# Dense attention with its softmax pairs joined one step earlier, squares taken tile by tile, and an output projection that opens two columns at once

## The reference

```
s = einsum(q, k) * d ** -0.5 ; causal                 # dense: 4 heads, each a pair of maps
p = softmax(s)
a = p[:, :, 0] - lam * p[:, :, 1]                      # the pair is joined
o = einsum(a, v)
y_c = rms(o, d_out_g) * (1 - lam_init)
merged = g0 * (y_a @ w0) + g1 * (y_b @ w1) + g2 * (y_c @ w2)
x = x + merged @ w_out
```

## Time and profile before

| | |
|---|---|
| median of three runs | 3001.89 us (3000.51 to 3002.13) |
| the profiled execution | 2999.98 us, its span 2998.2 us |
| granted TensorE clock | 0.998 of full speed |
| PE busy | 2944.5 us, 98% of the span |
| DVE, ACT, POOL busy | 1494.7, 674.4, 2001.7 us |
| PE in the chain that ended last | 91% |
| dense loop, layer 0 | about 276 to 382 us from the start, layer 1 about 1208 to 1313 |
| opening of the output projection | from 540.0 us, and from 1471.5 us |

### The profile page before, as it was taken

The page is one execution under the profiler, slowest core; times in us unless marked ns, Lnnn a source line. Parts: engine busy times, 40 slices in busy tenths (PEclk is TensorE's granted clock), DMA queues, the critical chain, the costliest instruction groups (busy, mean ns, idle before and its releaser), DMA issues.

```text
span 2998.2 us, 37823 instructions
## 1 busy us (share of the span) xinstructions
PE 2944.5 (98%) x13886; PEld 2402.7 (80%) x13886; DVE 1494.7 (50%) x2573; ACT 674.4 (22%) x1490; POOL 2001.7 (67%) x2041
## 2 busy tenths in 40 slices
PE   8999999999999999999999999999999999999998
PEld 6887777888888887777888888878888888888886
DVE  7778884533324788775543322566321231424543
ACT  3265354200001345345110000100111121211000
POOL 6775545777777767454777777887776556565775
PEclk9999999999999999999999999999999999999999
DMA  4321222333233322211433333233333223222332
GB/s 146 99 91 58 71 67 67 127 99 97 94 96 126 101 85 85 64 64 60 130 94 95 98 95 103 91 99 95 97 93 106 78 85 99 78 85 78 98 98 71
DMA packets 86922, 274.37 MB, mean 92 GB/s; under 512 B 10368, under 2 KB 11008, under 8 KB 86784
## 3 DMA queue, kind: packets, MB, share of 16 engines
q1 hardware_dynamic: 85248, 270.44, 29.1%
q10 hardware_dynamic: 1536, 2.10, 0.3%
HBM read 266.21 MB, written 4.19 MB: 90 GB/s over the span
## 4 chain that ended last, share of the span: by engine, by line
PE 91%; DVE 7%; ACT 1%; issue 1%; POOL 0%; DMA 0%; DVEq 0%; SPq 0%; ACTq 0%; POOLq 0%
PE PS L501 59%; PE PS L539 14%; PE PS L810 5%; PE PS L818 3%; PE PS L576 1%; PE PS L856 1%; PE PS L868 1%; PE PS L1107 1%; PE PS L897 1%; DVE SQ L1779 1%; PE PS L590 1%; PE PS L880 1%; DVE SMALLS L1744 0%; PE PS L1082 0%; PE PS L1094 0%
## 5 line engine op out<-in xcount | busy, mean ns | idle before, releaser
L471 POOL TENSOR_TENSOR WL<-RAW,WH 128x512 fp32r<-128x512 f32 (+2 forms) x538 | 803.4, 1493 | 9.8
L463 POOL TENSOR_TENSOR POOL_C<-POOL_C 128x1 f32<-128x1 f32 x538 | 127.1, 236 | 928.0 <-PE PS L501 517.7
L501 PE MATMUL PS<-XNH,WH 128*128 128x512 f32 (+1 forms) x1712 | 674.2, 394 | 1.5 <-DVE TMP L2342 1.2
L501 PE MATMUL PS<-XNL,WH 128*128 128x512 f32 (+1 forms) x1712 | 666.9, 390 | 0.0
L468 POOL TENSOR_TENSOR WL<-RAW,WH 128x512 fp32r<-128x512 f32 x420 | 578.1, 1377 | 35.0
L464 POOL TENSOR_SCALAR WH<-RAW 128x1024 fp32r<-128x1024 f32 (+3 forms) x538 | 533.4, 991 | 0.5 <-issue 0.3
L501 PE MATMUL PS<-XNH,WL 128*128 128x512 f32 (+1 forms) x1712 | 423.3, 389 | 0.1
L501 PEld LDWEIGHTS PS<-XNH,WH 128*128 128x128 f32 (+1 forms) x1712 | 320.8, 187 | 71.1 <-issue 5.0
L501 PEld LDWEIGHTS PS<-XNL,WH 128*128 128x128 f32 (+1 forms) x1712 | 320.9, 187 | 68.5 <-issue 2.2
L501 PEld LDWEIGHTS PS<-XNH,WL 128*128 128x128 f32 (+1 forms) x1712 | 320.5, 187 | 68.4 <-POOL WL L471 0.9
L539 PE MATMUL PS<-WH,XNH 128*128 128x512 f32 x704 | 279.4, 397 | 8.6 <-ACT TB L1207 6.8
(11 more groups left out here) (383 smaller groups left out, 4489.8 us busy)
## 6 DMA issues: line engine op xcount, KB each, us to landing
RAW<-w_oslot SPq DMA_DIRECT2D x56, 512.0 KB, 3.6
RAW<-w_L0ffn SPq DMA_DIRECT2D x44, 512.0 KB, 3.6
RAW<-w_L1ffn SPq DMA_DIRECT2D x44, 512.0 KB, 3.6
RAW<-w_od SPq DMA_DIRECT2D x32, 512.0 KB, 3.6
RAW<-w_L0G SPq DMA_DIRECT2D x24, 512.0 KB, 3.6
RAW<-w_L1G SPq DMA_DIRECT2D x24, 512.0 KB, 3.6
RAW<-w_epg SPq DMA_DIRECT2D x16, 512.0 KB, 3.6
RAW<-w_eug SPq DMA_DIRECT2D x16, 512.0 KB, 3.6
```

Of the source, the lines that this page charges most:

```text
L463: nc.gpsimd.tensor_tensor(POOL_C[:, 1:2], POOL_C[:, 0:1], POOL_C[:, 0:1], ALU.add)
L471: nc.gpsimd.tensor_tensor(WL[:, half, at_:w], RAW[:, slot, at_:w], WH[:, half, at_:w].bitcast(F32), ALU.subtract).then_inc(S("weights_spli ...
L501: mm = nc.tensor.matmul(bank, w[:, slot, k * cols:(k + 1) * cols], x[:, k0 + k, :], start=first and j == 0 and w is WH and x is hi, stop=l ...
```

## The change

VectorE's loop: the join moves into a function `join(q)` which is called in step q itself, behind `scale_gate(q + 1)` and ahead of the marks; before, it stood in step q + 1 behind the maxima. The squares of the normed output get a place of their own (SQA), ScalarE takes them tile by tile in steps 3, 5 and 7, and VectorE reduces tile n - 1 right behind the scaling of tile n. TensorE's last `values(7, 1)` moves behind the first sparse scores. The output projection's first two columns are opened together: six of eight tiles of the one, six of the other, then the last two of both, then the WL passes of both.

```diff
         def square_of(name, m, width):
             where = {"ckv": YC, "sq": YC, "dq": HALL, "sk": HALL, "h": YC}.get(name)
+            if name == "yc":
+                return SQA[:, 0:width]
...
                         if q < 8:
                             scores(q)
+                        if a and q == 0:
+                            values(7, 1)
...
                             if q < 8:
                                 branch(q)
-                            values(q - 1, 1)
+                                values(q - 1, 1)
...
-                         ready=lambda k: L("merged_ready", k + 1))
+                         ready=lambda k: L("merged_ready", k + 1), late=2)
...
+                def first_two():
+                    kt = pieces[0][0]
+
+                    def high(t, j):
+                        k = order[j]
+                        pe.wait_ge(*ready(j))
+                        for x in (hi, lo):
+                            nc.tensor.matmul(PS[banks[t]][:, :], WH[:, (c0 + t) % 2, k * P:(k + 1) * P], x[:, k, :],
+                                             start=j == 0 and x is hi, stop=False)
+
+                    for t in range(2):
+                        pe.wait_ge(S("high_ready"), c0 + t + 1)
+                        for j in range(kt - late):
+                            high(t, j)
+                    for t in range(2):
+                        for j in range(kt - late, kt):
+                            high(t, j)
+                    for t in range(2):
+                        pe.wait_ge(S("weights_split"), c0 + t + 1)
...
                         if q and a == 0:
                             for j in range(2):
                                 take_probs(j)
+                            if q in (3, 5, 7):
+                                square("yc", (q // 2 - 1,))
...
                     if a == 0:
-                        root("yc")
+                        square("yc", (3,))
+                        root("yc", squares=False)
...
+                def join(q):
+
+                    w = (q // 2 + 1) * P
+                    i0 = 8 * (q // 2 % 2) + 4 * (q % 2)
+                    dve.wait_ge(*L("att_e", 4 * q + 4))
+                    then(V.reciprocal(RS_[:, i0:i0 + 4], SUMS[:, i0:i0 + 4]))
+                    then(V.scalar_tensor_tensor(NLR[:, 0:2], RS_[:, i0 + 1:i0 + 4:2], LAM[:, 4:5],
+                                                SUMS[:, i0:i0 + 3:2], ALU.mult, ALU.mult))
+                    for j in range(2):
+                        first = SS[:, q % 2, 2 * j, 0:w]
+                        V.scalar_tensor_tensor(first, SS[:, q % 2, 2 * j + 1, 0:w],
+                                               NLR[:, j:j + 1], first, ALU.mult, ALU.add
+                                               ).then_inc(L("att_p"), 1)
...
                         if q < 8 and (a == 0 or q):
                             maxima_of(a, q)
-                        if q and a == 0:
-
-                            dve.wait_ge(*L("att_e", 4 * p + 4))
...
                         if a == 0 or q > 1:
                             scale_gate(q + 1 + 8 * a)
+                        if a == 0 and q < 8:
+                            join(q)
...
+                                if n:
+                                    squares(DA_HEADS, "yc", root=False, tiles=(n - 1,))
...
                         maxima_of(1, 0)
-                        squares(DA_HEADS, "yc")
+                        squares(DA_HEADS, "yc", tiles=(3,))
```

More of the change, by code:

```diff
@@ L219, in square_of @@
             where = {"ckv": YC, "sq": YC, "dq": HALL, "sk": HALL, "h": YC}.get(name)
+            if name == "yc":
+                return SQA[:, 0:width]
             if where is None:
-                at_ = m * T + (4 * T if name == "yc" else 0)
-                return MS[:, at_:at_ + width]
+                return MS[:, m * T:m * T + width]
             return where[:, m, 0:width]
@@ L985, in layer, with residual @@
                          ready=lambda k: L("hidden_ready", k + 1))
-            def residual(name, update, banks, pieces, hi, lo, order=None, ready=None):
+            def residual(name, update, banks, pieces, hi, lo, order=None, ready=None, late=0):
                 claim(*banks)
                 per, c0 = len(pieces), FIRST[name]
+                def first_two():
[15 more added lines that the diff above has]
+                        pe.wait_ge(S("weights_split"), c0 + t + 1)
+                        for j in range(kt):
+                            k = order[j]
+                            mm = nc.tensor.matmul(PS[banks[t]][:, :], WL[:, (c0 + t) % 2, k * P:(k + 1) * P],
+                                                  hi[:, k, :], start=False, stop=j == kt - 1)
+                        mm.then_inc(S("chunk_done"), 1)
                 def pair(i):
+                    if late and isinstance(i, int) and i == 0:
+                        first_two()
+                        return
                     for t in range(2):
@@ L1252, in chunk, with square @@
                     act.wait_ge(S("chunk_done"), c)
-                def square(name):
-                    for m in range(NT):
+                def square(name, tiles=range(NT)):
+                    for m in tiles:
                         i = 4 * (ROOT_NO[name] - 1) + m
@@ L1265, in square @@
                         if i >= NT:
-                            act.wait_ge(*L("square_used", i - NT + 1))
+                            act.wait_ge(*L("square_used", i if name == "yc" else i - NT + 1))
                         if name == "yc":
@@ L1737, in ask_root, with squares @@
                         then(V.reciprocal(RSH[:, 0:n], RSH[:, 0:n]))
-                def squares(h, name, keep=None, root=True):
-                    for n in range(NT):
+                def squares(h, name, keep=None, root=True, tiles=range(NT)):
+                    for n in tiles:
                         i, w = 4 * (ROOT_NO[name] - 1) + n, 256 if name == "ckv" else T
```

## The result

The changed kernel takes 3029.67 us, median of 6 runs (3026.68 to 3030.88); the kernel before, run beside it, 3001.2 us (2999.68 to 3002.13). The ratio is 1.0095 with a 95% interval of [1.0085, 1.0106]: slower by 28.5 us. The forecast was 3020 us, range 3004 to 3027. The direction was right; the loss is 1.5 times the 19.4 us of the sum, and 2.7 us outside the range.

What follows compares the result with a forecast made beforehand. TensorE, 98% busy, was taken as the bound, with no slack in step 3's chain to the first copy. Per layer 12.8 - 1.6 - 1.4 - 0.1 = 9.7 us more, 19.4 in both, gave 3020 us, range 3004 to 3027.

Steps and rivals of the forecast that it cites:

- the 19.4 us of the sum: Whole kernel: net loss forecast over both layers, 9.7 us more in each.
- The joins at the port: VectorE's moved joins meet GpSimd's split and wait in turn for SBUF: marks start 3.8 to 4.3 us later, by width.
- The new waits: Dense loop, steps 2 to 7: TensorE's values wait for ScalarE's late copy, 12.8 us a layer, against 1.6 that go.
- 12.8 - 1.6 - 1.4 - 0.1 = 9.7 us more: Per layer: new waits, less old transpose waits with slow starts, less the tail's gain, less the output projection's gain.
- The tail: Last values to transposes of y_c: two reductions leave and a slow start goes, gaining 1.4 us a layer (0.3 to 1.9).
- The output projection: Opening in pairs: TensorE waits 1.5 us for the second column's WH instead, gaining 0.1 us a layer (0 to 1.55).
- Faster: Rival: joins fit VectorE's idle time ahead of gate scalings, old waits go, 4.5 us a layer gained, 2993 us; chance 0.08.
- Free port: Rival: the port costs the joins nothing, J of 1.25 to 1.8 us, 2.2 us a layer more, 3006 us; chance 0.12.
- The looser lock: Rival: one join slips in ahead of POOL's second piece, 5.4 us a layer more, 3013 us; chance 0.15.
- 3027: Rival: VectorE also late at gate scalings, meeting GpSimd's next chunk, 3027 us; inside the 0.62 for 3014 to 3027.

Runs made afterwards that it cites:

- the run without the second SBUF input: Changed kernel with the factor and both joins taking one input from PSUM instead of SBUF, so y_c is not the reference's: 3008.08 us, ratio 1.0028.
- the run with filled waits: Changed kernel with 10, 13 and 14 extra 128x128 products ahead of the first values of steps 2, 5 and 7: 3021.87 us, ratio 1.0072.
- the run of the opening alone: Kernel before the change with only the output projection's first two columns opened in pairs: 3001.75 us, ratio 1.0001.

## Why the prediction was right in kind and short in size

**The joins at the port: right.** Whole instructions exclude each other in turn, in the changed kernel as in the one pair that the trace of before held; the run without the second SBUF input takes it away.

**The new waits: right in sum, not in every pair.** 12.8 us a layer were forecast against 1.6 that go, 11.2 net; measured is 10.6 and 11.3 of idle time. By pairs:

| pair | forecast | layer 0 | layer 1 |
|---|---|---|---|
| steps 2 and 3 | 3.9 | 2.60 | 3.91 |
| steps 4 and 5 | 4.6 | 5.48 | 4.91 |
| steps 6 and 7 | 4.3 | 3.64 | 3.63 |

The first pair holds in layer 1. In layer 0 its missing 1.3 us went into the clock. Both layers wait alike in step 2 (2.60 and 2.59 us), and VectorE and ScalarE then need the same time. But in layer 0 the clock falls behind the wait, TensorE loses 1.7 us, reaches the values of step 3 that much later and finds their copy there:

```profile
321.47 0.60 PE L881 MATMUL PS<-DV,TB 128*128 128x128 f32 x4
```

In layer 1 the clock stays full and TensorE waits 1.32 us there. From the values of step 2 to those of step 3 it is 11.99 us in the one and 11.91 in the other.

The second pair has a lock that the sum left out. The prediction says of MAX8 and the replacing of marks, with one input from SBUF, that they run beside GpSimd at their usual length, and it puts no other one-input instruction into the chain. The TENSOR_SCALAR that closes each group of rounds has one input too, and in step 4 of layer 0 it meets a piece of GpSimd's next split:

```profile
339.69 1.40 DVE L2085 TENSOR_SCALAR MSK<-MSK 128x256 f32<-128x256 f32 x1
```

```profile
339.67 1.27 POOL L472 TENSOR_TENSOR WL<-RAW,WH 128x512 fp32r<-128x512 f32 x1
```

It takes 0.29 us alone, so 1.1 us come on top of the chain. In layer 1 the sign change of step 5, of four numbers a row, meets a first piece and takes 0.89 us for 0.17 (at 1291.94). What made the third pair 0.7 us shorter than forecast stays open.

VectorE, once late, also reaches the join before its own exponentials are done and waits for them (0.81, 0.98 and 1.24 us in steps 2, 4 and 5 of layer 0). The join then starts when part of the split is over and waits less for it.

**The step that failed: "12.8 - 1.6 - 1.4 - 0.1 = 9.7 us more".** The sum held waits only, and priced TensorE's work behind each of them at its old length, although it allowed 0.15 us of slow start for the short waits that went. Behind three of the four waits in layer 0 and two of the five in layer 1 the clock falls, each time with some 1.7 us of work lost; the same 487 matmuls take 5.2 us longer in layer 0 and 3.9 in layer 1. Not all of it is added to the time, since a slow stretch can take the place of a wait: the run with filled waits has the loops at full clock and is 4.84 + 3.24 = 8.1 us shorter in them. That the 19.4 us of the sum and the 9.1 us of longer busy time make just the 28.5 measured is luck, since the tail gained 1.2 us less than forecast over both layers and the waits were 0.5 us shorter.

**The tail: 1.4 forecast, 0.8 measured.** From the end of the last gate chunk of the loop to the transposes of y_c it was 10.53 us (377.66 to 388.19) and is 9.72 (393.21 to 402.93). SQA is one buffer; tile 3's square waits for tile 2's reduction, and a table load of 1.28 us stands behind it. The forecast had counted reductions and had not followed the squares' buffer. By the run with a buffer of its own, that is 0.4 of the missing 0.6; the rest stays open.

**The output projection: right.** The wait of 1.4 us for the second column's weights is where it was put (PE L1002 in the table of waits), and the run of the opening alone shows no gain. The 0.1 us itself is too small to measure.

**The rivals.** "Faster" fell as argued: idle time ahead of a scaling is no room for the join. "Free port" (3006) is near what the run without the second input gave, 3008, of which some part is again the clock. The looser lock never showed. 3027, VectorE late at its scalings too, was nearest in number, but not by its mechanism alone: in layer 0 it is late there in steps 2 and 5, by 0.8 and 0.9 us (in step 2 it starts at 307.80, where GpSimd started at 307.03 on the same signal), in layer 1 by 0.8 and 1.8.

## What to carry to other kernels

Before an instruction with two SBUF inputs is moved on VectorE, look what GpSimd does in the place where it goes: one that meets a piece of a split, even one of two numbers, waited here for the end of that piece (up to 1.33 us for the factor, 0.22 alone). A one-input TENSOR_SCALAR was held up as well. A step that comes late by tenths may start to meet the split every time. A chain that runs around a loop over several engines has a room of its own (here copy after scaling 10.16 us against 10.07); idle time on one engine in it is not that room. Where a change opens waits of 2 to 4 us on TensorE, the slower matmuls behind them are a term of their own: here 8 us on top of 23, by the run with filled waits.

## What the runs showed of the hardware

- TensorE's granted clock did not follow the length of a wait alone. In the changed kernel it fell behind 2.60 us in layer 0 (0.73 from 309.40 on) and stayed full behind 2.59 us in layer 1 (the first line below). In the kernel with the join ahead of the scaling it fell behind 1.84 us (the second line), where 2.06 us did nothing in the changed kernel.

```profile
1255.88:1262.00 6.12, 6.12 (x32) 4.86 (x33) 5.78 (x15) 0.89 (x2) 3.41 (x5) 1.00 0.25 87
335.60:341.00 5.40, 5.40 (x21) 4.45 (x22) 5.26 (x10) 1.10 (x2) 2.06 (x3) 0.68 0.32 97
```

- Ahead of the loop too the clock differed. Behind a wait of some 3.5 us that both kernels have at 240 us, the changed kernel ran at 0.66 from 240 to 245 us and the kernel before at 1.00, though the change edits nothing that runs there (before, then changed).

```profile
240.00:245.00 5.00, 4.86 (x21) 4.05 (x22) 3.94 (x7) 3.96 (x9) 0.00 (x0) 1.00 0.05 20
```

```profile
240.00:245.00 5.00, 5.00 (x15) 3.98 (x16) 4.12 (x8) 3.96 (x9) 0.00 (x0) 0.66 0.03 13
```

- A one-input TENSOR_SCALAR of VectorE, from SBUF to SBUF, and a piece of GpSimd's split held each other up too: 128 x 256 took 1.40 us in the changed kernel and 1.44 with the opening alone, each beside a piece, and 0.29 in the kernel before. The starts on record don't tell which of the two goes first. In the kernel before, VectorE's is at 332.73 and GpSimd's at 332.75, and it took 0.29 while the piece took 1.42; with the opening alone they are at 333.91 and 333.93, and it took 1.44 while the piece took 1.27.

What decides whether the clock falls stays open; per wait it is a matter of 0 or about 1.7 us, so a forecast of such a sum has to carry a range.
